# Alternating full and light expert visits, with a fourth light visit, in a transformer trunk on one core

## The reference, cut to what matters

```python
def moe_swiglu(h, router, w_in, w_out):
    logits = jnp.einsum('bnd,de->bne', h, router).astype(jnp.float32)
    top_logit, top_idx = lax.top_k(logits, TOP_K)            # 2 of 8 experts for each of 256 tokens
    top_w = jax.nn.softmax(top_logit, axis=-1)
    gates = jnp.sum(jax.nn.one_hot(top_idx, N_EXPERTS, dtype=jnp.float32) * top_w[..., None], axis=-2)
    out = jnp.zeros_like(h)
    for e in range(N_EXPERTS):
        out = out + gates[..., e:e + 1].astype(h.dtype) * swiglu(h, w_in[e], w_out[e])
    return out
```

## Time and profile before

| | before |
|---|---|
| median of 3 runs | 2006.77 us (2005.42 to 2007.82) |
| the profiled execution, its time | 2000.83 us |
| its span | 1998.0 us |
| PE busy | 1799.9 us, 90% of the span |
| DVE, ACT, POOL busy | 900.9, 755.9, 328.6 us |
| read from HBM | 468.18 MB |

### The profile page before, as it was taken

How to read it: one execution, slowest core, us unless ns; L and a number is a source line. 1 busy time by engine, 2 the same in 40 slices (tenths; PEclk the granted TensorE clock), 3 DMA queues, 4 the chain that set the end, 5 groups by cost and what they waited for, 6 DMA issues and landing times. The chain is left out here.

```text
span 1998.0 us, 22229 instructions
## 1 busy us (share of the span) xinstructions
PE 1799.9 (90%) x8552; PEld 1253.0 (63%) x8561; DVE 900.9 (45%) x1052; ACT 755.9 (38%) x791; POOL 328.6 (16%) x118
## 2 busy tenths in 40 slices
PE   3898789999999978977999999999999999898984
PEld 1566477777778776466887877878866653332431
DVE  1237432222233452537887878878855531010102
ACT  2223442122122444435766766757645520000001
POOL 0100011100101120012432433333312210000000
PEclk9998789999999988988999999999999999999998
DMA  8770214544432231115998989989857779999994
GB/s 336 262 274 1 84 63 163 195 169 169 169 148 71 79 122 45 42 54 183 363 348 294 362 310 344 368 281 364 325 192 249 237 239 358 396 392 395 394 394 182
DMA packets 194750, 470.30 MB, mean 235 GB/s; under 512 B 8457, under 2 KB 34034, under 8 KB 188018
## 3 DMA queue, kind: packets, MB, share of 16 engines
q1 hardware_dynamic: 191474, 463.32, 64.2%
q10 hardware_dynamic: 3200, 5.96, 0.8%
HBM read 468.18 MB, written 1.07 MB: 235 GB/s over the span
## 5 line engine op out<-in xcount | busy, mean ns | idle before, releaser
L239 DVE TENSOR_TENSOR low<-raw,high 128x2048 fp32r<-128x2048 f32 (+3 forms) x268 | 546.0, 2056 | 395.7 <-ACT high L231 391.2
L231 ACT ACTIVATE high<-raw 128x2048 fp32r<-128x2048 f32 (+1 forms) x268 | 509.6, 1903 | 503.3 <-PE PS L260 333.2
L239 POOL TENSOR_TENSOR low<-raw,high 128x1024 fp32r<-128x1024 f32 (+1 forms) x89 | 293.0, 3292 | 1124.1 <-ACT high L231 1124.1
L258 PE MATMUL PS<-high,ah 128*128 128x512 f32 (+2 forms) x1030 | 413.4, 401 | 16.9 <-DVE low L239 7.8
L260 PE MATMUL PS<-high,al 128*128 128x512 f32 (+2 forms) x1030 | 401.4, 390 | 0.0
L259 PE MATMUL PS<-low,ah 128*128 128x512 f32 (+2 forms) x1030 | 401.2, 390 | 0.0
L258 PEld LDWEIGHTS PS<-high,ah 128*128 128x128 f32 x1030 | 195.5, 190 | 97.1 <-issue 31.3
L260 PEld LDWEIGHTS PS<-high,al 128*128 128x128 f32 x1030 | 195.3, 190 | 40.7
L259 PEld LDWEIGHTS PS<-low,ah 128*128 128x128 f32 x1030 | 195.8, 190 | 36.2
L1996 PE MATMUL PS<-raw,work 128*64 128x512 f32 (+1 forms) x896 | 185.0, 601 | 21.2 <-DMA raw<-in_moe_w_in_dram 18.8
L258 PE MATMUL PS<-ah,high 128*128 128x512 f32 (+1 forms) x392 | 153.7, 392 | 2.5 <-issue 2.5
(11 more groups left out here) (282 smaller groups left out, 1524.5 us busy)
## 6 DMA issues: line engine op xcount, KB each, us to landing
raw<-in_moe_w_in_dram SPq DMA_DIRECT2D x224, 1024.0 KB, 7.7
raw<-in_moe_w_out_dram SPq DMA_DIRECT2D x112, 1024.0 KB, 8.0
raw<-in_ada_w_dram SPq DMA_DIRECT2D x48, 1024.0 KB, 7.9
raw<-in_ffn_w_in_dram SPq DMA_DIRECT2D x22, 1024.0 KB, 5.1
raw<-in_ffn_w_out_dram SPq DMA_DIRECT2D x11, 1024.0 KB, 5.0
raw<-in_ab_w_in_dram SPq DMA_DIRECT2D x8, 1024.0 KB, 7.6
raw<-in_ab_w_out_dram SPq DMA_DIRECT2D x4, 1024.0 KB, 7.2
raw<-in_mla_w_o_dram SPq DMA_DIRECT2D x4, 1024.0 KB, 4.9
```

What stands on the lines that cost most here:

```text
L231: act.activation(high[n % SPL][:, 0:width], raw[u % RAW][:, 0:width], ACT.Copy).then_inc(high_made, 1)
L239: eng.tensor_tensor(low[n % SPL][:, c0:c1], raw[slot(n) % RAW][:, c0:c1], high[n % SPL][:, c0:c1].bitcast(F32), ALU.subtract).then_inc(low ...
L258: pe.matmul(o, sh, mh, start=start, stop=False)
```

## The change

The order of the kinds becomes H L H L H L X L. The fourth largest of experts 1 to 7 now gets a light visit (`LEAST` replaces the rank from which the cap is 64), so there are four L visits, three H visits and one X visit. The biggest expert is still the X visit. L visits now have H and X behind them, so they make their tokens and split the first three units for them. The late loop runs four times instead of three, and where there is no late visit only DVE does anything: one increment of `acc_made`.

```diff
-NLATE = TOP * SEQ // (P + 1)
+NLATE = 4
-KIND = "HHHHXLLL"
-RANK = [None, 1, 2, 3, 0, 4, 5, 6]
+KIND = "HLHLHLXL"
+RANK = [None, 6, 1, 5, 2, 4, 0, 3]
+LEAST = 3
...
             # SP, late loop
                 with sp.If(some > 0):
                     late_visit(j + NE, j + FULLS[NE], e)
-                with sp.Else():
-                    for u in range(slot(N_MOE), slot(N_MOE) + 6):
-                        r = u % RAW
-                        sp.wait_ge(raw_loaded[r], 16 * (u // RAW) + (j + NE) * (16 * NCH))
-                        sp.sem_inc(raw_loaded[r], 16 * NCH)
...
             # ACT
-            def light_visit(l):
+            def light_visit(v, l, h, nxt):
                 light_gate("L", l, 0)
                 with act.Fori(0, NCH - 1) as i:
                     light_silu("L", l, i)
                     light_gate("L", l, i + 1)
                 light_silu("L", l, NCH - 1)
+                if nxt in ("H", "X"):
+                    split_high(act, U0, counts(v + 1, h))
+                    for hf in range(2):
+                        tokens(h, hf)
+                    for j in range(1, 3):
+                        split_high(act, U0 + j, counts(v + 1, h))
...
-                with act.Else():
-                    act.wait_ge(high_made, N_MOE + h * VISIT)
-                    act.sem_inc(high_made, VISIT)
-                    for name, k in (("xg_high", 2), ("esilu_made", NCH), ("ht_high", NCH)):
-                        act.wait_ge(s[name], h * k)
-                        act.sem_inc(s[name], k)
...
             # DVE
-                link(dve.tensor_scalar(cap, key, top[:, 4:5], -float(P - GROUP["L"]), ALU.is_le, ALU.mult))
+                link(dve.tensor_scalar(cap, key, top[:, LEAST:LEAST + 1], -float(P - GROUP["L"]), ALU.is_le, ALU.mult))
...
                 light_hidden("L", l, NCH - 1)
-                if nxt:
+                if nxt in ("H", "X"):
+                    for hf in range(2):
+                        scaled(h, hf)
+                    low_units(U0, h * NCH, (0,))
+                    for hf in range(2):
+                        tokens(h, hf)
+                if nxt in ("X", "L"):
                     light_tokens(nxt, l + 1)
                 gated("L", v, 0, l)
+                if nxt in ("H", "X"):
+                    low_units(U0, h * NCH, (1, 2))
...
                 with dve.Else():
-                    for sl in range(SPL):
-                        m = makers(sl)
-                        before = m * len([n for n in range(N_MOE) if n % SPL == sl])
-                        dve.wait_ge(low_made[sl], before + h * (2 * NCH * m))
-                        dve.sem_inc(low_made[sl], 2 * NCH)
-                    for name, k, n, more in (("sel_made", 1, v, 0), ("xg_scaled", 2, h, 0), ("xg_ready", 2, h, 0), ("selt_copied", 1, v, 0),
-                                             ("h_made", NCH, h, 0), ("ht_ready", NCH, h, 0), ("y_gated", 1, v, 0), ("acc_made", 1, v, 1)):
-                        dve.wait_ge(s[name], n * k + more)
-                        dve.sem_inc(s[name], k)
+                    dve.sem_inc(s["acc_made"], 1)
...
             # PE, light visit
                     downs(8, i)
-                if nxt:
+                if nxt in ("H", "X"):
+                    gather(v + 1, h)
+                if nxt in ("X", "L"):
                     light_gather(nxt, v + 1)
```

More of the change, by code:

```diff
@@ L860, in _ @@
                         pool_low(pool, first + 3, (j + FULLS[NE]) * NCH + i)
-                with pool.Else():
-                    pool.wait_ge(low_made[SPL - 1], 2 * (first // SPL) + (j + FULLS[NE]) * (4 * NCH))
-                    pool.sem_inc(low_made[SPL - 1], 2 * NCH)
             res_pool(pool, 3)
@@ L1096, in _ @@
                 if KIND[v] == "L":
-                    light_visit(LIGHTS[v])
+                    light_visit(v, LIGHTS[v], FULLS[v], (KIND + " ")[v + 1])
                 else:
@@ L1563, in visit, with light_visit @@
                     accumulate(v)
-            def light_visit(v, l, nxt, e):
+            def light_visit(v, l, h, nxt, e):
                 accumulate(v - 1)
@@ L1595, in _ @@
                 if KIND[v] == "L":
-                    light_visit(v, LIGHTS[v], nxt, e)
+                    light_visit(v, LIGHTS[v], FULLS[v], nxt, e)
                 else:
@@ L2123, in visit, with light_visit @@
                     scatter(v, kind)
-            def light_visit(v, l, nxt):
+            def light_visit(v, l, h, nxt):
                 def ups(idx, chunks, parts=(0, 1)):
@@ L2157, in _ @@
                 if KIND[v] == "L":
-                    light_visit(v, LIGHTS[v], nxt)
+                    light_visit(v, LIGHTS[v], FULLS[v], nxt)
                 else:
@@ L2168, in _ @@
                     visit(v, h, 0, "H", "")
[L2169 to L2174, removed]
 _INS = ['x', 'c', 'ctx', 'c_ctx', 'ada_w', 'ada_b', 'g_pre_mix', 'g_post_mix', 'g_pre_ffn', 'g_post_ffn',
```

## The result

The changed kernel takes 1987.43 us (median of 4 runs, 1978.30 to 1988.29) beside 2006.10 us of the kernel before (4 runs, 2004.61 to 2007.82). The ratio is 0.9897, interval 0.9881 to 0.9914: by it 1.03% or 20.7 us faster (17 to 24). I had forecast faster, by 9.4 us. The sign was right; the size was less than half of what was measured.

The account below looks back on a forecast made before the run. PE was taken to bound H and X visits, transfers L visits. Visits -15.2, late loop -2.0 and clock +7.8 us gave -9.4, so a median of 2006.77 becomes 1997.4 us; range 1986 to 2005.

Parts of the forecast that it names:

- the limits and the exchange: Expert visits: PE sets H and X, transfers set L; a full visit costs about 20 us more than a light one.
- L behind H: L visits following an H visit: only a full scatter part ahead, so 111.5 us each, for two of them.
- the starts of H: H behind L: PE starts 2.9 us late, scatter saves 1.7; from the H mean of 132.05 to 133.3 us, twice.
- The L visit ahead of X: The L visit before the X visit makes both gathers, the second for 3.66 us: 115.1 us.
- the late loop: End of program, before the final norm: four cheaper passes instead of three, 2 us saved.
- two models: Late loop: DVE sequencer walks on during adds, 0.16 us a pair, 3.1 us saved; or it does not, 0.07, nothing saved.
- the term for the clock behind the new gaps: PE's idle gaps ahead of H and X behind L: clock falls at X and one H, 7.8 us lost, bounds 0 and 12.1.
- the sum without a clock term: Visits 1 to 7: 925.4 us before, 910.2 after, 15.2 us less.
- no clock fall: Rival: the new gaps ahead of H and X bring no fall, -17.2 us, 1989.6 us; chance 0.20.
- Three falls with a loss of 12.1 us: Rival: all three gaps ahead of H and X bring the clock down, -5.1 us, 2001.7 us; chance 0.20.
- run dry: Rival: H and X behind L start without 5 us of cover, first units wait for transfers, 2013 us; chance 0.08.
- head start of six loads: Rival: H leaves L six loaded units, up to 12 us less in each of three L visits, about 1975; chance 0.06.

Follow-up runs that it names:

- grouped order: The changed kernel with its four light visits in a row, order H H H X L L L L: 1979.55 us, ratio 0.9884; run again, 1979.03 us, ratio 0.9883.
- new late loop: The kernel before with only the Else branches of the change, three passes and visit order unchanged: 1998.98 us, ratio 0.9977.
- old late loop: The changed kernel with the Else branches of all five engines put back, four passes: 1991.02 us, ratio 0.9943.
- changed kernel again: The changed kernel without any edit, measured a second time against the kernel before: 1983.25 us, ratio 0.9897.
- gap filled: The changed kernel with ten matmuls of zeros behind each L visit that has an H visit next: 1983.41 us, ratio 0.9893.

## Why the prediction was right or wrong

**Right: the limits and the exchange.** H behind PE, L behind the transfers; no late visit (336 loads again). L behind H: 111.5 forecast, 111.5 and 111.9 measured. The last L visit 110.3 and 110.3. The grouped order has the exchange without new hand-overs: 23 us with the new late loop.

**Right in mechanism, small in error: the starts of H.** An H visit behind L is 131.9 us without a fall (old late loop, changed kernel again), forecast 133.3: the gap is 2.30 us and not 2.9, and my base of 132.05 already had a clock fall in one of its two visits.

**Off at X, with errors that cancelled in part.** The L visit ahead of X took 118.7 us (forecast 115.1), X 194.5 (195.2 before any clock term). I had written that L visits can hardly lose by the clock, and put the fall into X, behind a gap of 4.7 us. The clock fell ahead of the hand-over in all five profiles; the last units of L took 5.1 to 6.6 us for 3.65, and the gap behind them was only 1.12 to 2.63 us. The gathers are not the cause by themselves: the H visit ahead of X makes the same 64, and in none of the eight profiles that have one was the clock low there. In the kernel before, in the columns of the earlier trace rows:

```profile
1434.16:1441.60 7.44, 7.44 (x69) 7.43 (x67) 7.34 (x13) 3.77 (x4) 0.25 (x1) 1.00 1.02 375
```

**Right by luck: the late loop.** 2.0 us forecast, 1.99 measured (10.65 to 8.66). It was a value between two models, and neither is right: a fourth pass cost 2.83 us with the new loop (5.83 to 8.66) and 4.43 with the old (10.65 to 15.08). So the eleven pairs of wait and increment cost 1.6 us a pass, and the three passes of 10.65 and 5.83 us give the same 1.6. That is 0.15 each, as in the first model, but the first passes cost less than the fourth.

**Wrong: the term for the clock behind the new gaps, +7.8 us.** This is the step that failed. I charged 10.1 us at half clock for a gap, from the 3.21 us one; behind the ten gaps of 2.3 to 2.9 us there were 3.4 us in 7 cases, worth 1.3 us each, and filling the gap gained nothing that a comparison shows. And I charged it on the changed kernel only, with the kernel before at nothing more than its one profile had. The kernel before has falls at its own waits of 1.5 to 2.0 us, four waits in a profile's visits 1 to 4, of which the changed order keeps three: 5 of 12 had a fall in or right behind them in its three profiles, and 5 of 12 in the four profiles of the changed order. Its visits took 5.7 us longer in the profile of the new late loop. Over the profiles, by DVE's gated results, the visits of the kernel before take 925.1, 925.4 and 930.8 us, mean 927.08. Those of the changed order (changed kernel twice, by 1047.60 to 1963.09 and 1049.41 to 1959.06, old late loop, gap filled by 1049.20 to 1960.04) take 915.5, 909.7, 909.4 and 910.8, mean 911.35. The difference is 15.7 us, where the sum without a clock term had 15.2: the falls cost about as much before as after, and the net term is near nothing. Without the 7.8 the sum gives 17.2 us less, the case that I had called "no clock fall" at 0.20, but for another reason: falls came. The measured interval of 17 to 24 us begins there.

**The rest.** 3 to 4 us between that sum and the ratio are not explained term by term, and stay open. The first profiled execution of before lay 3 us under the median of 40 later runs, and I carried its distance to the median over unchanged. That a single profile stands for a kernel whose runs spread over 10 us was the weak assumption.

**The rivals.** Three falls with a loss of 12.1 us did not come; 7 falls behind 10 gaps at 1.3 us are about a third of the price for each that I had made. The Trainium skill (TensorE: Matmul & The Clock Gate, "Why this matters for your kernels") warns of idle gaps of PE between bursts of matmuls that are longer than any of these ten. The seven falls show that here a shorter gap was no assurance of a full clock. H did not run dry behind L: PE's later wait in the visit stayed at 1.50 us. The head start of six loads was not seen, L behind H took the 111.5 us.

## What to carry to other kernels

Read the cost of a kind of stage and of each hand-over between kinds apart; here putting a transfer-limited stage in the place of a compute-limited one took 16 us off the visits (19 in the grouped order, by the means of the profiles), and their alternation gave nothing. If a cost comes at random places, such as a fall of the clock behind short waits, count how often it comes in the kernel before too, in more than one profile, before charging it to the change. And a loop that only finds out that it has nothing to do is serial work at the end of a program: one test ahead of it took 6.3 us off the end of both profiles that have it.

## What the runs showed of the hardware

A wait of PE of 1.5 to 2.9 us had 3.4 or 6.8 us at granted clock 0.50 in or right behind it in some executions and nothing in others, at the same place of the same program; at two places in visit 0 all 13 profiles agree, with no fall at a gap of 2.85 us and one at a gap of 1.51 us. In the L visit ahead of X, 64 small gather matmuls (128x128 and 128x32) ran without a gap of note, and the clock fell to 0.50 at their end or up to 2.3 us behind it, for 3.4 to 10.2 us, in all five profiles that have it. The same 64 in an H visit had no fall in eight profiles, so what else differs between the two visits has a part in it; which part, no run shows. Ten bf16 matmuls of zeros (2.33 us) filled the 2.30 us gap without any delay of the work behind.
